# A retention and window-attention trunk: first chunk in halves, two pieces of combining work moved, four low parts made by VectorE

## What is computed

```
h  = x + retention(rmsnorm(x)) @ w_out      # 4 heads, q/k 256 wide, v and gate 512 wide
     # retention: rope(q), rope(k); o = masked(q k^T) v + q R; R = decay R + k^T v
     # o normed per head; y = o * silu(g)
kv = rmsnorm(h) @ w_kv                      # 2 kv heads, 64 wide, rotary
h  = h + swa(rmsnorm(h) @ w_in, kv, sinks) @ w_swa_out   # 16 heads, window 128, silu gate
out = rmsnorm(h)
```

## Time and profile before

| | |
|---|---|
| runs | 2436.65, 2438.07, 2438.33 us |
| profiled execution | 2439.43 us, span 2437.6 us, granted clock 0.998 |
| PE | 2390.0 us busy, 98% of the span |
| DVE | 1503.8 us, 62% |
| ACT | 680.0 us, 28% |
| POOL | 454.4 us, 19% |
| DMA | 625.85 MB, mean 257 GB/s |
| chain that ended last | PE 90%, DVE 7%, issue 1%, DMA 1%, ACT 1% |

### The profile page before, as it was taken

The page is one execution under the profiler, slowest core; times in us unless marked ns, Lnnn a source line. Parts: engine busy times, 40 slices in busy tenths (PEclk is TensorE's granted clock), DMA queues, the critical chain, the costliest instruction groups (busy, mean ns, idle before and its releaser), DMA issues.

```text
span 2437.6 us, 28654 instructions
## 1 busy us (share of the span) xinstructions
PE 2390.0 (98%) x11216; PEld 1964.5 (81%) x11216; DVE 1503.8 (62%) x2042; ACT 680.0 (28%) x1470; POOL 454.4 (19%) x322
## 2 busy tenths in 40 slices
PE   7999999999999999999999999999999999999998
PEld 6888888877887787878888888888888787888886
DVE  6554655567766777763767564565567745647384
ACT  2312212235221212232533121232352212313243
POOL 2111111221345665640010010100001101101000
PEclk9999999999999999999999999999999999999999
DMA  8667575654899999974379877775357977786433
GB/s 354 264 242 287 195 275 207 256 192 165 320 402 378 363 372 356 364 298 173 104 253 324 278 257 254 266 248 207 122 198 243 330 257 266 248 289 238 173 104 147
DMA packets 131834, 625.85 MB, mean 257 GB/s; under 512 B 8864, under 2 KB 9632, under 8 KB 109728
## 3 DMA queue, kind: packets, MB, share of 16 engines
q1 hardware_dynamic: 122864, 588.53, 66.8%
q10 hardware_dynamic: 8880, 36.18, 4.0%
HBM read 471.58 MB, written 153.09 MB: 256 GB/s over the span
## 4 chain that ended last, share of the span: by engine, by line
PE 90%; DVE 7%; issue 1%; DMA 1%; ACT 1%; POOL 0%; DVEq 0%; SPq 0%; POOLq 0%; ACTq 0%
PE ps L709 29%; PE ps L711 28%; PE ps L710 28%; PE ps L1219 2%; DVE ff L2288 1%; PE ps L1229 1%; DVE fr L1678 1%; PE ps L1027 1%; PE ps L857 1%; DVE mx L2328 1%; DMA whl<-comb_w 1%; DVE xlo L1678 0%; DVE ff L2358 0%; DMA raw<-in_stream 0%; PE ps L1159 0%
## 5 line engine op out<-in xcount | busy, mean ns | idle before, releaser
L709 PE MATMUL ps<-whl,xhi 128*128 128x512 f32 (+1 forms) x1088 | 416.7, 383 | 2.3 <-DVE xlo L1678 2.3
L711 PE MATMUL ps<-whl,xlo 128*128 128x512 f32 (+1 forms) x1088 | 411.5, 378 | 0.0
L710 PE MATMUL ps<-whl,xhi 128*128 128x512 f32 (+1 forms) x1088 | 410.4, 377 | 0.0
L709 PE MATMUL ps<-xhi,whl 128*128 128x512 f32 x768 | 303.8, 396 | 17.6 <-DVE xlo L1682 16.2
L711 PE MATMUL ps<-xhi,whl 128*128 128x512 f32 x768 | 300.2, 391 | 0.0
L710 PE MATMUL ps<-xlo,whl 128*128 128x512 f32 x768 | 299.5, 390 | 0.0
L709 PE MATMUL ps<-whl,fr 128*128 128x512 f32 x640 | 256.9, 401 | 5.6 <-DMA whl<-comb_w 3.2
L711 PE MATMUL ps<-whl,fr 128*128 128x512 f32 x640 | 254.5, 398 | 0.0
L710 PE MATMUL ps<-whl,fr 128*128 128x512 f32 x640 | 254.0, 397 | 0.0
L709 PEld LDWEIGHTS ps<-whl,xhi 128*128 128x128 f32 x1088 | 204.9, 188 | 40.1 <-issue 3.1
L711 PEld LDWEIGHTS ps<-whl,xlo 128*128 128x128 f32 x1088 | 204.7, 188 | 38.6
(11 more groups left out here) (214 smaller groups left out, 3854.0 us busy)
## 6 DMA issues: line engine op xcount, KB each, us to landing
whl<-split_w SPq DMA_DIRECT2D x60, 2048.0 KB, 8.2
whl<-split_w SPq DMA_DIRECT2D x118, 1024.0 KB, 6.9
split_w<-whl SPq DMA_DIRECT2D x44, 2048.0 KB, 7.2
whl<-vg_w SPq DMA_DIRECT2D x64, 1024.0 KB, 6.9
raw<-in_stream SPq DMA_DIRECT2D x44, 1024.0 KB, 9.4
vg_w<-ff SPq DMA_DIRECT2D x32, 1024.0 KB, 10.3
whl<-comb_w SPq DMA_DIRECT2D x32, 1024.0 KB, 6.5
raw<-in_stream SPq DMA_DIRECT2D x50, 512.0 KB, 10.4
```

The source lines that it names most:

```text
L709: pe.matmul(dst, lhs[0], rhs[0], start=start, stop=False)
L710: pe.matmul(dst, lhs[0], rhs[1], start=False, stop=False)
L711: return pe.matmul(dst, lhs[1], rhs[0], start=False, stop=stop)
```

## The change

It does four things. Chunk 0 is loaded, rounded and split in two halves, the half for k = 4 to 7 first (`LEAD` is 1024 columns), with the low parts of x made between the halves; PE waits for the second half only at its fifth k. The fifth piece's low part moves on DVE behind two more `add_product`. The sixth rows' load moves on SP from behind the store of the c = 6 turn to behind the c = 7 loads. The low parts of y's four sums move from GpSimd to DVE in all twelve heads of blocks 1 to 3.

```
# SP
-                sp.dma_start(raw[n % 2][:, 0:width(n)], raw_source(n)).then_inc(w_loaded[n % 2].sem, 16)
+                if n == 0:
+                    sp.dma_start(raw[0][:, LEAD:CHUNK], stream[0:P, LEAD:CHUNK]).then_inc(lead_loaded.sem, 16)
+                    sp.dma_start(raw[0][:, 0:LEAD], stream[0:P, 0:LEAD]).then_inc(w_loaded[0].sem, 16)
+                else:
+                    sp.dma_start(raw[n % 2][:, 0:width(n)], raw_source(n)).then_inc(w_loaded[n % 2].sem, 16)
...
                     if c == 6:
                         store_lo(3)
+                        store_hi(4)
+                    else:
                         load_piece(h, 5)
-                        store_hi(4)
# GpSimd
-            round_chunk(0)
+            pool.wait_ge(lead_loaded.sem, 16)
+            pool.tensor_scalar(whi[0][:, LEAD:CHUNK], raw[0][:, LEAD:CHUNK], 1.0, 1.0, ALU.mult, ALU.mult).then_inc(lead_hi.sem, 1)
+            pool.wait_ge(w_loaded[0].sem, 16)
+            pool.tensor_scalar(whi[0][:, 0:LEAD], raw[0][:, 0:LEAD], 1.0, 1.0, ALU.mult, ALU.mult).then_inc(w_hi.sem, 1)
...
-                    y_sums_lo(at)
...
-                y_sums_lo(Place("head", BLOCKS - 1, h))
# PE, chunk 0 of the first head
+                        if begin and c == 0:
+                            pe.wait_ge(lead_ready.sem, 1)
+                        else:
+                            w_wait(at, c)
...
+                                if begin and n == 4:
+                                    w_wait(at, c)
# DVE, start
-            split_chunk(0)
-            for n in range(KT):
+            dve.wait_ge(lead_hi.sem, 1)
+            dve.tensor_tensor(wlo[0][:, LEAD:CHUNK], raw[0][:, LEAD:CHUNK], whi[0][:, LEAD:CHUNK].bitcast(F32), ALU.subtract).then_inc(lead_ready.sem, 1)
+            for n in range(4):
+                next_lo(at, 0, n)
+            dve.wait_ge(w_hi.sem, 1)
+            dve.wait_ge(lead_ready.sem, 1)
+            dve.tensor_tensor(wlo[0][:, 0:LEAD], raw[0][:, 0:LEAD], whi[0][:, 0:LEAD].bitcast(F32), ALU.subtract).then_inc(w_ready[0].sem, 16)
+            for n in range(4, KT):
                 next_lo(at, 0, n)
# DVE, both kinds of head
+                    def sum_lo(a):
+
+                        dve.wait_ge(a_hi.sem, at(a_hi, HI_ORDER.index(a) + 1))
+                        less_hi(ahl[a][1], asum[a], ahl[a][0], s_parts_lo)
# DVE, fast_head
                     add_product(0, 2, 0, 1)
+                    sum_lo(S1)
                     y_sum(S3)
                     part_lo(A11)
                     y_sum(S2)
                     part_lo(A12)
                     y_sum(S4)
+                    sum_lo(S3)
+                    sum_lo(S2)
+                    sum_lo(S4)
# DVE, combining head
                         add_product(2, 2, 0, 1)
+                        sum_lo(S1)
                         y_sum(S3)
                         part_lo(A11)
                         y_sum(S2)
                         part_lo(A12)
                         y_sum(S4)
-                        if combine:
-                            comb_less_hi(at, 4)
+                        sum_lo(S3)
+                        sum_lo(S2)
+                        sum_lo(S4)
                         dve.wait_ge(p_mm.sem, at(p_mm, 2))
                         add_product(0, 2, 1, 1)
                         add_product(0, 0, 1, 1)
+                        if combine:
+                            comb_less_hi(at, 4)
                         dve.wait_ge(p1_copied.sem, at(p1_copied, 1))
                         add_sum(0, 0, 0, 1)
```

More of the change, by code:

```diff
@@ L55 @@
 CHUNK = 2048
+LEAD = CHUNK // 2
 HEAD_CHUNKS = 8
@@ L233, in build @@
         w_ready = [count(f"w_ready{i}", head=4, post=7, unit=16) for i in range(2)]
+        lead_loaded = count("w_lead_loaded")
+        lead_hi = count("w_lead_hi")
+        lead_ready = count("w_lead_ready")
         w_stored = [count(f"w_stored{i}", head=4, post=7, unit=16) for i in range(2)]
@@ L670, in x_sums_lo @@
                     pool.tensor_tensor(xpart[a][1], xsum[a], xpart[a][0].bitcast(F32), ALU.subtract).then_inc(x_part_lo.sem, 1)
[L672 to L676, removed]
             for b in range(1, BLOCKS - 1):
@@ L747, in one_head @@
                     for c in (0, 1):
-                        w_wait(at, c)
+                        if begin and c == 0:
+                            pe.wait_ge(lead_ready.sem, 1)
+                        else:
+                            w_wait(at, c)
                         if c == 1:
```

## The result

The kernel before took 2438.33 us (median of 5 runs, 2436.65 to 2439.09), the changed one 2450.45 us (5 runs, 2447.90 to 2453.52): ratio 1.0051, 95% interval 1.0039 to 1.0063. The forecast was 2447.0 us in a range of 2442 to 2453, and slower. The profiled execution after took 2453.52 us, its span 2451.7: 3.1 us above its median, where that of before was 1.1 us above. So of the 14.1 us between the two spans about 12 stand in the medians.

The account below looks back on a forecast made before the run. TensorE, busy 98% of the span, was taken as the bound. Blocks 2 and 3 +8.6, block 1 +1.8 and the first chunk -1.5 gave +8.9 us, from the median 2438.07 to 2447.0 us, range 2442 to 2453.

Parts of the forecast that it names:

- Low part of S1, blocks 2 and 3: Eight heads: product S1 starts 1.07 us later, its low part standing behind an add on DVE; +8.6 us.
- Block 1: All four heads of block 1 together: -2.7 + 1.5 + 1.5 + 1.5 = +1.8 us.
- the lost drop behind T2: First head of block 1: slow clock after the wait for the second transposed rows goes, 1.5 us expected back.
- S1: Block 1: product S1 starts 1.70 us later, its low part standing behind the add on DVE.
- S3: Block 1, heads 2 and 3: the 1.20 us wait before product S3 goes, -1.20 a head.
- First head: First head of block 1: second transposed rows (T2) arrive earlier, slow clock behind their wait goes; -2.7 us, bounds -3.5 and 0.
- A12: Block 1, heads 2 and 3: product A12 waits for the first grow_sum; +1.0 us a head, between +0.4 and +1.7.
- End of block: Last head of block 1: sixth piece's rounding comes later and DVE's chain is longer; +1.5 us, bounds 0 and +2.5.
- Rival 1: Clock drops after block 1's S1 waits and the start's 2.7 us wait; +7.5 us on top, 2454.5; chance 0.10.
- First chunk: Start: first product 4.3 us earlier, mean squares' row at 27.15 instead of 28.66; -1.5 us, bounds -4.3 and 0.
- Sum: Whole kernel: 8.6 + 1.8 - 1.5 = +8.9 us, span from 2437.6 to 2446.5.

Follow-up runs that it names:

- e2: The changed kernel with S1's low part on DVE ahead of the first add instead of behind it; 2443.00 us, ratio to before 1.0022.
- e5: The kernel before with only the load of the sixth piece's rows moved behind the second transposed rows; 2435.68 us, ratio to before 0.9994.
- e1: The changed kernel with the four low parts of y's sums back on GpSimd; 2432.77 us, ratio to before 0.9976.
- e3: The kernel before with only the first chunk in halves; 2435.52 us, ratio to before 0.9992.
- e7: The changed kernel with e2's move and the fifth piece's low part behind the first grow_sum; 2435.34 us, ratio to before 0.9988.
- e10: e1 with the root of the mean squares ahead of the work on chunk 1 on GpSimd and DVE; 2433.04 us, ratio to before 0.9980.
- e6: The kernel before with only the fifth piece's low part moved behind the two adds into hres; 2441.35 us, ratio to before 1.0018.
- e4: The kernel before with only the four low parts of y's sums moved to DVE; 2458.58 us, ratio to before 1.0080.

## Why the prediction was right, and what in it was off

**Low part of S1, blocks 2 and 3: right.** Predicted 1.07 us a head and 8.6 in all; the waits are 1.11, the rest of the span grew by 8.9, and e2 shows that the position behind the add is the cause and that the three other low parts are free, as said.

**Block 1: mis-sized, +5.3 instead of +1.8.** From head to head, between TensorE's first transposes of each, the four parts changed by -2.4, +1.8, +4.0 and +1.9 (109.94, 105.82, 105.84 and 102.52 us before; 107.52, 107.59, 109.86 and 104.44 after), against -2.7, +1.5, +1.5 and +1.5. The mis-sized term is the clock. The forecast counted the lost drop behind T2 as -1.5 and no new one; measured are one drop before and two after, +1.7. Without the clock the forecast was +3.3 and the measurement is +3.6, and that near agreement is in part luck, as the last two heads show.
- S1: +1.70 was forecast; the start of S1 moved from 0.16 to 1.88 us behind the add, +1.72 (the idle time in brackets is 1.48). Right. But the waits don't add up as the sum assumed: e2 took them away and block 1 gained 0.2. Half of S1's delay was time that TensorE would have spent at A12, where VectorE's list is the bound; most of the other half it would have spent waiting for loads in the first head and for VectorE's last adds in the last.
- S3: its wait went, as forecast. First head: T2's wait went with the low clock behind it, as forecast; e5 shows that the load's move does this alone.
- A12: +1.0 was taken in heads two and three, and the waits are 1.21 and 1.99. The sum took one operation held up; in heads three and four two were, the fifth piece (3.08 and 3.18 us) and the add behind it (2.31). The Trainium skill (SBUF — State Buffer, Who interferes with whom) has the pair of ports taken in turn for an instruction's whole length. GpSimd was first by 0.27 and 0.37 us, and 2.31 against 1.22 is a whole hold-up, not a slowing in proportion, so the trace agrees. The forecast's low bound, +0.4 if VectorE comes first, failed too: in the second head VectorE is first, and the hold-up falls on the add behind the piece.
- End of block: +1.5 was forecast for a longer wait at the last transposes. That wait shrank instead, from 2.54 to 0.32. The time is lost earlier, in an A12 wait of 2.09 that the forecast had not put into this head and in a clock drop of 1.7. That the head comes to +1.9 is luck.
- Rival 1, the clock, came true in part: not behind any of the twelve S1 waits, nor behind the start's 1.59, but behind the A12 waits of 1.99 and 2.09, for 3.4 us. The prediction took 2.54 us as safe from one case, and passed over a wait of 2.1 us in the same trace, for `whl` L1720, that ends at 588.36. The stretch behind it, in the kernel before:

```profile
590.00:595.00 5.00, 5.00 (x20) 4.09 (x19) 2.55 (x7) 1.37 (x7) 0.00 (x0) 0.73 0.98 331
```

**First chunk: -0.3 instead of -1.5 in this pair of profiles, and right by number over all of them.** The first half landed at about 10.3 instead of 8.5, since the smaller rows got the smaller share of the queues; the first product started at 13.47 instead of 11.9. The forecast had said that nothing around the root moves; `hres` and chunk 1 landed 0.9 and 1.1 us later (17.71 and 22.00, from 16.80 and 20.88), and the root with them. Where `xms` was not held (e1, e2, e3, e7) the row came at 27.0 to 27.1, the forecast's number, but by luck: loads 0.4 to 0.8 us later and a root 2.1 us shorter cancel. The low parts do nothing before the row, so these four have the changed kernel's start; the four traces with the start of before have the row at 28.66, 29.94, 29.10 and 29.28. The means are 29.25 and, with the changed kernel's 28.37, 27.32: a gain of 1.9, and e3's median has 2.0. So most of the missing 1.3 us looks like chance in one profile of each kernel; how often the changed kernel's start comes out on the slow side the runs don't show.

**Sum.** By the landmarks: -0.1 up to block 1, +5.3 in it, +8.9 behind, 14.1 us of span; the forecast was +8.9. In block 1 3.5 us were missed, 3.2 of them the clock; the 1.4 up to it are mostly the one profile. With a gain of about 2 us in the start, an estimate from the rows and medians above, the parts come to 12, and the medians differ by 12.1. The median stayed in the range because that reached almost to rival 1.

## What to carry to other kernels

Before an operation is moved to another engine, look at what stands ahead of it in that engine's list when the waiting engine needs it: here the same 0.68 us an operation cost 8.9 us over eight heads behind an add and nothing ahead of it. If an edit shifts a transfer, look which two instructions of GpSimd and VectorE it brings side by side, since a hold-up of whole instructions falls on the next link of the chain. Do not add up the waits of one chain: taking 5.9 us of them away gained 0.2. And measure edits apart: three of these four were worth 5 us together, and one of those three was a loss by itself.

## What was not expected of the hardware

- **A wait of about 2 us may or may not cost the clock.** TensorE's idle time, and the lowest granted clock of the stretches of 5 us around its end: 1.80, 0.81 (e7); 1.84, 0.83 (e10); 1.99, 0.66; 2.09, 0.72; 2.06 and 2.57, 0.81 and 0.66 (e6); 2.52 and 2.55, 0.68 and 0.66 (e2); 2.79, 0.50 (e4). But after 1.92 (twice) and 2.58 (e4), 2.04 (e6, twice), 2.52 (e2, in another head) and 2.54 it stayed at 1.00. No wait of 1.67 us or less was seen with a lower clock behind it in any of the eleven traces, and none of 2.79 or more (3.02 in e3, 3.25, 3.90 in e7) without; the one of 2.1 that ends near 588 had it in all eleven. What decides in between stays open. A drop costs 1.7 us (0.95 and 0.71 over two stretches of 5 us in the trace before, 735 to 745), the one of 0.50 twice that.
- **The first matmuls run at the pace of the lower clock for a time that differs from run to run.** In the trace before their distance falls from 0.43 to 0.23 us at 19.31, in that of e4, whose start is the same code, at 22.22 (timeline of each):

```profile
18.90 0.57 PE L709 MATMUL ps<-xhi,whl 128*128 128x512 f32 x1
19.31 0.39 PE L710 MATMUL ps<-xlo,whl 128*128 128x512 f32 x1
```

```profile
21.93 0.46 PE L703 MATMUL ps<-xlo,whl 128*128 128x512 f32 x1
22.22 0.39 PE L704 MATMUL ps<-xhi,whl 128*128 128x512 f32 x1
```

  The row came at 28.66 and 29.94 accordingly. A gain of a us in the start can't be read from one profile of each kernel. The profile before had the shortest of these phases, so it also makes the halves look worse than they are.
- **Small operations are held too.** `xms`, 512 values with one input, took 1.93 instead of 0.17 us when GpSimd's rounding had begun 0.01 us earlier; in e2, with 0.002 us between them, it took 0.17. The copy of the root took 1.89 (e10).
